# A three-block layer at width 1024: the order of TensorE's queue at the norm boundaries

## The chip, the cores and the metric

One core of a Trainium2 chip runs the whole program. The metric is the device time of one execution in microseconds (us); the median of several executions stands for a kernel.

## The reference

A sequence of 512 tokens of width 1024 passes two blocks, all in fp32. Every projection is preceded by an RMS norm, whose statistic is a mean of squares over the 1024 features of a token.

```
# first block (16 meta tokens are put in front of the 512)
h = concat([meta, x])
z = rmsnorm(h) @ w_in                      # a, q, k, v, r, lr, ga, gb
y_a = (pool means of a, mixed per group) @ w_pool_out
o = gated linear attention(q, k, v, lr)    # chunks of 64, 4 heads
o = rmsnorm(o) * silu(r);  y_b = o @ w_gla_out
h = h + (sigmoid(ga) * y_a + sigmoid(gb) * y_b) @ w_out
h = h + square(relu(rmsnorm(h) @ w_ff1)) @ w_ff2
x = rmsnorm(h)[16:]
# second block
p = rmsnorm(x) @ w_in_first                # convolution branch and RWKV-7 branch
x = x + rmsnorm(concat([conv(p), rwkv7(p)]) @ w_out)
x = x + rmsnorm(cross attention(rmsnorm(x), mem) @ wo)
x = x + rmsnorm(swiglu(rmsnorm(x)))
```

## The kernel before, in words

Activations lie with features on the partitions: F(i) is a slot of 128 features by 512 tokens. A weight matrix is streamed in units of up to 128 x 2048 values by SyncE, into two raw buffers. Each unit is split by ScalarE (a rounded copy, `wh`) and VectorE (the remainder, `wl`) in pieces of 1024 columns; activations are split the same way, and a product of 128 x 128 by 128 x 512 is made of three matmuls. So a tile (128 output features, 8 steps of k) is 24 matmuls, and a tile of `go` (4 steps of k) is 12. The three matmuls stand in `dense`.

`schedule()` writes one list of steps, and every engine walks it and issues those steps for which it has a function. The order on each engine is thus fixed by hand. `tile` puts the two halves of a tile's matmuls and then its eviction (`ev.<tag>`); `pair` puts two tiles with k as the outer loop, and `pair_end` their evictions. `next_unit` starts a unit: it puts the loads of the two units behind it and the splits of this unit and the next one. Background work (pooling, gated linear attention, convolution taps, the RWKV recurrence, cross attention) is made of generators, and `step` moves each by some yields after every half tile; `drain` runs them to their end. `take` and `rel` hand out the eight PSUM banks in turn, D for dense tiles and M for background work; the first matmul into a bank waits for the eviction of the bank's last user.

A norm is not applied to the operand but to the output of the next projection, so that the dense tiles need not wait for it; their evictions do. A statistic has four parts. ScalarE squares a feature tile, and GpSimd adds the squares into one 128 x 512 sum (`squares`, `add_squares`). `cols` lets TensorE sum over partitions, with 8 short instructions of one column each; VectorE adds epsilon and GpSimd takes the power of -1/2. `spread` lets TensorE lay the result out over all partitions (8 matmuls of 128 columns), and ScalarE copies it to SBUF, where the evictions read it.

The places that the change touches:

- The start: pair 0 of unit `a`, the narrow matmuls of the 16 meta columns (`mmm`, 24 for each tile), `in.rs` (the statistic of the tokens) and `in.rm` (that of the meta columns).
- The boundary `gb` to `go`: after `drain`, the four steps `og` multiply the attention output by its gate (VectorE), round it (ScalarE) and make the remainder (VectorE): the operands `in.os` of `go`. The eviction `ev.go` is a VectorE multiply, a GpSimd add, a ScalarE copy and a VectorE remainder, which is the operand `in.m` of `wo`; SyncE then reloads x into the slot.
- The boundary `wo` to `f1`, with the statistic `ffn.rs`.
- The boundary `f2` to `p`, with `mid.a` and `mid.b`; the second is the norm of a normed value, and `midb` combines the two on VectorE and GpSimd. The steps `x2` scale the eight slots on VectorE, and SyncE stores them.

Of the kernel before, what the change touches and what calls it, by code (L numbers as in the profile page):

```python
# [178 lines left out]
class Plan:  # L179


    def __init__(self):
        self.steps, self.bank, self.before = [], {}, {}
        self.pools = {"D": [0, 1, 2], "M": [3, 4, 5, 6, 7]}
        self.user = {}
        self.done = set()
        self.bgs, self.pace, self.rate, self.weight = [], {}, 1, {}
        self.unit, self.loaded, self.cut = 0, set(), set()
        self.base = {}
        for n, u in enumerate(UNITS):  # L190
            self.base.setdefault(u[0], []).append(n)
# [9 lines left out]
    def rel(self, pool, *key):  # L201
        self.pools[pool].append(self.bank[key])

# [70 lines left out]
    def pair(self, n, i0, meta=False):  # L274
        tag = UNITS[n][0]
        for j in range(2):
            self.take("D", "t." + tag, i0 + j)
        for k in range(UNITS[n][3]):
            self.put("ko", n, i0, k)
        if meta:  # L280
            for j in range(2):
                self.take("M", "t." + tag + "_m", i0 + j)
                self.put("mmm", n, j, i0 + j)

    def pair_end(self, n, i0, meta=False):
        tag = UNITS[n][0]
        for j in range(2):
            self.put("ev." + tag, i0 + j)
            if meta:
                self.rel("M", "t." + tag + "_m", i0 + j)  # L290
            self.rel("D", "t." + tag, i0 + j)
            self.step()
# [12 lines left out]
def schedule():  # L305
# [9 lines left out]
    def bg_gla():  # L315
# [58 lines left out]
        for h in range(4):  # L374
            put("gla.sq", h)
            yield
            pl.cols(f"gla.n{h}", "M")
            yield
            pl.spread(f"gla.n{h}", "M")
            put("gla.norm", h)  # L380
            yield

# [8 lines left out]
    for k in range(8):  # L391
        put("sq.in", k)
    n = pl.next_unit("a")
    pl.pair(n, 0, meta=True)
    pl.cols("in.rs")
    pl.spread("in.rs")
    pl.cols("in.rm")
    pl.spread("in.rm")
    pl.pair_end(n, 0, meta=True)
# [22 lines left out]
    pl.drain(bgm)  # L422
    pl.begin(bg_gla())
# [28 lines left out]
    for tag, cnt in (("r", 2), ("ga", 4), ("gb", 4)):  # L452
        for uu in range(cnt):
            n = pl.next_unit(tag)
            for j in range(2):
                pl.tile(n, j, 2 * uu + j)
    pl.drain()
    for h in range(4):
        put("og", h)
# [4 lines left out]
    for uu in range(4):  # L464
        n = pl.next_unit("wo")
        for j in range(2):
            pl.tile(n, j, 2 * uu + j)
    put("gfg")
    for g in range(4):
        for uu in range(4):  # L470
            n = pl.next_unit("f1")
            i0 = 8 * g + 2 * uu
            if g == 0 and uu == 0:
                pl.pair(n, i0)
                pl.cols("ffn.rs")
                pl.spread("ffn.rs")
                pl.pair_end(n, i0)
# [16 lines left out]
    pl.spread("mid.a")  # L494
    pl.cols("mid.b")
    put("midb")
    pl.spread("mid.b")
    put("cvz")
    put("pset")
    pl.pair_end(n, 0)  # L500
    p_tile(0)
    p_tile(1)
# [193 lines left out]
    due = None  # L696
    for uu in range(1, 7):
# [130 lines left out]
    def one_bank_set():  # L828
        pl.pools["D"] += pl.pools["M"]
        pl.pools["M"] = []  # L830

    one_bank_set()
# [49 lines left out]
    pl.pools["M"], pl.pools["D"] = pl.pools["D"][3:], pl.pools["D"][:3]  # L882
# [14 lines left out]
    one_bank_set()  # L897
# [45 lines left out]
def program(nc, wstream, vecs, cf, cu, xT, metaT, memT, pmix, gup, wau, gupg, out, x2s, kvs):  # L943
# [5 lines left out]
    with ctx:  # L949
# [718 lines left out]
        def scalar(e):  # L1668
# [20 lines left out]
            def sq_in(k):  # L1689
                squares("in.rs", k, F(k))  # L1690
                squares("in.rm", k, mh[:, k, :])
# [308 lines left out]
            def evh_dn(i, h):  # L2000
# [4 lines left out]
                "split": split, "xs": xs, "ms": ms, "sq.in": sq_in, "spread": spread, "gla.gate": gla_gate,  # L2005
# [530 lines left out]
        def gpsimd(e):  # L2536
# [14 lines left out]
            def sq_in(k):  # L2551
                add_squares("in.rs", k)
                add_squares("in.rm", k)
# [102 lines left out]
            def end_b(_, i, h):  # L2656
# [5 lines left out]
                "cols": cols, "sq.in": sq_in, "gla.prod": gla_prod, "ev.r": ev_r, "ev.ga": ev_ga, "ev.go": ev_go,  # L2662
# [185 lines left out]
```

How the kernel before makes its waits and increments, by code:

```python
    def wait_ge(self, *keys):  # L136
        for key in keys:
            if key is None or self.value is None:
                continue
            sem, n = self.value[key]
            if n > self.seen.get(sem, 0):
                self.seen[sem] = n
                self.raw.wait_ge(self.book.handle(sem), n)
# [1109 lines left out]
            def dense(n, j, b, k, x, N, done=None, c0=0):  # L1253
                _, _, _, nk, _, w, _ = UNITS[n]
                b = b[0:w, c0:c0 + N]
                c = (j * nk + k) * w
                lh, ll = WH[n % 2][:, c:c + w], WL[n % 2][:, c:c + w]
                xh, xl, key = x
                e.wait_ge(("w.lo", n, min(c // 1024, len(cut_list(n)) - 1)), key)
                e.mm(b, lh, xh, start=(k == 0), stop=False)
                e.mm(b, lh, xl, start=False, stop=False)
                t = e.mm(b, ll, xh, start=False, stop=(k == nk - 1))
                if done and k == nk - 1:
                    t.then_inc(*e.up("mm", *done))
# [1 line left out]
            def mm(n, j, i, half):  # L1266
                tag, nk = UNITS[n][0], UNITS[n][3]
                K = ("t." + tag, i)
                if half == 0:
                    e.wait_ge(freed(*K))
                for k in range(nk // 2) if half == 0 else range(nk // 2, nk):
                    dense(n, j, ps(*K), k, operand(tag, i, k), 256 if tag == "km" else 512, K)
# [20 lines left out]
            def mmm(n, j, i):  # L1293
                K = ("t." + UNITS[n][0] + "_m", i)
                e.wait_ge(freed(*K))
                for k in range(8):
```

## Time and profile before

| | us |
|---|---|
| Median of three executions | 1794.6 |
| The three | 1794.26, 1794.6, 1799.52 |
| The profiled execution | 1800.14 |
| Its span, first to last instruction | 1798.0 |
| TensorE busy | 1678.5 |
| VectorE busy | 834.5 |
| ScalarE busy | 604.5 |
| GpSimd busy | 402.2 |

The profiled execution is one of its own, and the device time beside its span has some 2 us of start and end around it. Busy times overlap. The mean granted clock of TensorE over the span was 0.955 of full speed.

### The profile page before, as it was taken

How to read it: one execution, taken by the hardware profiler on the slowest of the kernel's cores; microseconds unless marked ns; L12 is line 12 of the kernel's file. 1: busy time of each engine (PE TensorE's matmuls, PEld its weight loads, DVE VectorE, ACT ScalarE, POOL GpSimd, SP SyncE). 2: the span in 40 equal slices, each digit the busy share in tenths (PEclk: the TensorE clock that was granted, in tenths of full speed). 3: DMA queues.
4: the chain of work that ended last, by engine and by line, in shares of the span. 5: the costliest groups of instructions: out<-in, count | busy, mean ns of one | idle time of the engine just before them, and what ended most of it. 6: DMA issues, size and time to landing. Idle time of an engine off the chain costs nothing.

```text
span 1798.0 us, 26861 instructions
## 1 busy us (share of the span) xinstructions
PE 1678.5 (93%) x11510; PEld 1377.9 (77%) x11510; DVE 834.5 (46%) x1240; ACT 604.5 (34%) x973; POOL 402.2 (22%) x349
## 2 busy tenths in 40 slices
PE   7999999989999999998988877898989899999997
PEld 6789878767788888887776666777859878888876
DVE  3468642345333333344556887635633433233234
ACT  4234332223323232343335442324433423222222
POOL 2102111112201010132034540104203432131133
PEclk8899999999999999998999889898999999999998
DMA  6124311223222222222311100013202222222221
GB/s 213 48 71 147 136 71 47 94 71 117 84 104 87 101 90 98 93 85 90 120 49 48 47 3 2 3 49 131 81 24 71 71 94 94 94 94 94 94 76 65
DMA packets 29829, 146.03 MB, mean 81 GB/s; under 512 B 4096, under 2 KB 7440, under 8 KB 14608
## 3 DMA queue, kind: packets, MB, share of 16 engines
q1 hardware_dynamic: 29712, 144.33, 22.8%
q8 instruction: 91, 1.49, 0.4%
q14 instruction: 26, 0.21, 0.0%
HBM read 138.03 MB, written 6.29 MB: 80 GB/s over the span
## 4 chain that ended last, share of the span: by engine, by line
PE 77%; issue 8%; DVE 7%; POOL 5%; ACT 3%; DMA 0%; POOLq 0%; SPq 0%; DVEq 0%; ACTq 0%
PE ps L153 77%; POOL zf L165 4%; DVE zf L165 2%; DVE zf L173 2%; ACT zf L162 1%; ACT zf L159 1%; POOL tn L165 1%; DVE ps L173 1%; DVE wl L165 1%; ACT zr L162 1%; ACT wh L162 0%; PE ps L156 0%; DVE zf L2292 0%; DMA raw<-in_wstream 0%; DVE zr L173 0%
## 5 line engine op out<-in xcount | busy, mean ns | idle before, releaser
L153 PE MATMUL ps<-zr,wh 128*128 128x512 f32 (+1 forms) x3936 | 1181.6, 385 | 34.0 <-DVE wl L165 13.4
L153 PEld LDWEIGHTS ps<-zr,wh 128*128 128x128 f32 x3936 | 722.4, 192 | 197.0 <-issue 13.3
L153 PE MATMUL ps<-zr,wl 128*128 128x512 f32 (+1 forms) x1968 | 748.9, 381 | 0.0
L165 POOL TENSOR_TENSOR zf<-zf 128x512 f32<-128x512 f32 (+1 forms) x253 | 297.1, 1181 | 869.1 <-ACT zf L159 581.4
L153 PEld LDWEIGHTS ps<-zr,wl 128*128 128x128 f32 x1968 | 376.5, 191 | 77.6
L165 DVE TENSOR_TENSOR wl<-raw,wh 128x1024 fp32r<-128x1024 f32 (+1 forms) x243 | 306.2, 1300 | 231.9 <-ACT wh L162 231.9
L162 ACT ACTIVATE wh<-raw 128x1024 fp32r<-128x1024 f32 (+1 forms) x243 | 240.3, 1037 | 198.4 <-PE ps L153 196.8
L159 ACT ACTIVATE zf<-zf 128x512 f32<-128x512 f32 (+2 forms) x232 | 127.6, 560 | 411.7 <-DVE zf L165 297.2
L153 PE MATMUL ps<-zf 64*64 64x64 f32 (+6 forms) x3640 | 204.1, 248 | 34.6 <-DVE zf L165 18.6
L153 PEld LDWEIGHTS ps<-zf 64*64 64x64 f32 (+3 forms) x3640 | 162.8, 149 | 75.7 <-issue 29.7
L165 DVE TENSOR_TENSOR zf<-ps,zf 128x512 f32<-128x512 f32 (+2 forms) x133 | 84.2, 639 | 214.1 <-PE ps L153 198.3
L162 ACT ACTIVATE zf<-ps 128x512 f32<-128x512 f32 (+2 forms) x160 | 74.1, 482 | 205.2 <-PE ps L153 189.9
L165 POOL TENSOR_TENSOR zr<-zf,zr 128x512 fp32r<-128x512 f32 x54 | 69.8, 1293 | 285.8 <-ACT zr L162 285.8
L165 DVE TENSOR_TENSOR zf<-zf,ps 128x512 f32<-128x512 f32 (+1 forms) x112 | 62.7, 571 | 147.8 <-PE ps L153 146.6
L162 ACT ACTIVATE zr<-zf 128x512 fp32r<-128x512 f32 x74 | 46.4, 631 | 172.9 <-POOL zf L165 144.2
L153 PE MATMUL ps<-cf_sb,zf 64*64 64x64 f32 (+2 forms) x988 | 68.3, 242 | 23.9 <-ACT zf L159 13.2
L153 PEld LDWEIGHTS ps<-cf_sb,zf 64*64 64x64 f32 (+1 forms) x988 | 63.9, 165 | 28.2 <-issue 11.7
L165 POOL TENSOR_TENSOR tn<-tn,cf_sb 128x2 f32<-128x2 f32 (+3 forms) x29 | 31.6, 1090 | 222.7 <-DVE tn L169 130.5
L173 DVE SCALAR_TENSOR_TENSOR zf<-ps,zf 128x512 f32<-128x512 f32 x46 | 31.4, 690 | 98.2 <-PE ps L153 90.8
L162 ACT ACTIVATE zf<-zf,vecs_sb 128x512 f32<-128x512 f32 x73 | 49.7, 716 | 52.4 <-DVE zf L165 44.9
L173 DVE SCALAR_TENSOR_TENSOR zr<-zf,vecs_sb,zr 128x256 fp32r<-128x256 f32 (+1 forms) x64 | 45.5, 720 | 44.6 <-ACT zr L162 44.6
L165 DVE TENSOR_TENSOR zf<-zf 128x512 f32<-128x512 f32 (+4 forms) x91 | 59.6, 666 | 11.3 <-ACT zf L159 10.2
(94 smaller groups left out, 720.2 us busy)
## 6 DMA issues: line engine op xcount, KB each, us to landing
raw<-in_wstream SPq DMA_DIRECT2D x117, 1024.0 KB, 4.8
zf<-in_xT SPq DMA_DIRECT2D x16, 256.0 KB, 2.8
raw<-in_wstream SPq DMA_DIRECT2D x4, 768.0 KB, 4.3
kv_scratch<-zf SPq DMA_DIRECT2D x8, 256.0 KB, 2.2
x_scratch<-zf SPq DMA_DIRECT2D x8, 256.0 KB, 2.1
zf<-x_scratch SPq DMA_DIRECT2D x8, 256.0 KB, 4.5
out<-zf SPq DMA_DIRECT2D x16, 128.0 KB, 1.7
zf<-in_cu SPq DMA_DIRECT2D x1, 1256.0 KB, 9.9
```

Source lines behind the costliest of these rows:

```text
L153: return self.raw.matmul(out_, l, x, start=start, stop=stop)
L159: return self.raw.activation(out_, in_, fn, bias=bias, scale=scale)
L162: return self.raw.activation(out_, in_, mybir.ActivationFunctionType.Copy, scale=scale)
L165: return self.raw.tensor_tensor(out_, a, b, o)
L173: return self.raw.scalar_tensor_tensor(out=out_, in0=a, scalar=s, in1=b, op0=o1, op1=o2)
```

## The change

Bank sets: all eight PSUM banks serve dense tiles where no background work with PSUM runs (from the start to the end of `q`, and from `go` through the first two units of `p`), where before three did. `two_bank_sets` and `one_bank_set` switch.

The start: the squares of the tokens are all made before those of the meta columns, on ScalarE and GpSimd. The column sums of `in.rs` stand right behind the first pair, and the narrow matmuls of the two tiles stand between the statistics' steps.

`og` is made by the background generator of the attention, one head a step, once `r` is there. The first two tiles of `wo` are a `pair`.

`ffn.rs`, `mid.a` and `mid.b`: after the first pair the column sums follow at once, and the spreads are put between the half tiles of the second unit, whose matmuls now stand ahead of the first pair's evictions. So four tiles wait for their evictions there. `x2` stands behind the evictions of four `p` tiles instead of two.

```diff
@@ -181,7 +181,7 @@
 
     def __init__(self):
         self.steps, self.bank, self.before = [], {}, {}
-        self.pools = {"D": [0, 1, 2], "M": [3, 4, 5, 6, 7]}
+        self.pools = {"D": list(range(8)), "M": []}
         self.user = {}
         self.done = set()
         self.bgs, self.pace, self.rate, self.weight = [], {}, 1, {}
@@ -200,6 +200,13 @@
 
     def rel(self, pool, *key):
         self.pools[pool].append(self.bank[key])
+
+    def two_bank_sets(self):
+
+        self.pools = {"D": self.pools["D"][:3], "M": self.pools["D"][3:]}
+
+    def one_bank_set(self):
+        self.pools = {"D": self.pools["D"] + self.pools["M"], "M": []}
 
     def mark(self, *key):
         self.done.add(key)
@@ -271,23 +278,17 @@
         self.rel("D", "t." + tag, n, i)
         self.step()
 
-    def pair(self, n, i0, meta=False):
+    def pair(self, n, i0):
         tag = UNITS[n][0]
         for j in range(2):
             self.take("D", "t." + tag, i0 + j)
         for k in range(UNITS[n][3]):
             self.put("ko", n, i0, k)
-        if meta:
-            for j in range(2):
-                self.take("M", "t." + tag + "_m", i0 + j)
-                self.put("mmm", n, j, i0 + j)
-
-    def pair_end(self, n, i0, meta=False):
+
+    def pair_end(self, n, i0):
         tag = UNITS[n][0]
         for j in range(2):
             self.put("ev." + tag, i0 + j)
-            if meta:
-                self.rel("M", "t." + tag + "_m", i0 + j)
             self.rel("D", "t." + tag, i0 + j)
             self.step()
 
@@ -379,6 +380,11 @@
             pl.spread(f"gla.n{h}", "M")
             put("gla.norm", h)
             yield
+        while not has(("r",)):
+            yield
+        for h in range(4):
+            put("og", h)
+            yield
 
     put("pro")
     for k in range(8):
@@ -388,15 +394,22 @@
             pl.split(0)
     for k in range(8):
         put("ms", k)
-    for k in range(8):
-        put("sq.in", k)
+    for what in ("sq.in", "sq.im"):
+        for k in range(8):
+            put(what, k)
     n = pl.next_unit("a")
-    pl.pair(n, 0, meta=True)
+    pl.pair(n, 0)
     pl.cols("in.rs")
-    pl.spread("in.rs")
-    pl.cols("in.rm")
+    for j in range(2):
+        pl.take("D", "t.a_m", j)
+        put("mmm", n, j, j)
+        if j == 0:
+            pl.cols("in.rm")
+            pl.spread("in.rs")
     pl.spread("in.rm")
-    pl.pair_end(n, 0, meta=True)
+    pl.pair_end(n, 0)
+    for j in range(2):
+        pl.rel("D", "t.a_m", j)
     n = pl.next_unit("a")
     for j in range(2):
         pl.tile(n, j, 2 + j, meta=True)
@@ -420,6 +433,7 @@
     for j in range(2):
         pl.tile(n, j, j)
     pl.drain(bgm)
+    pl.two_bank_sets()
     pl.begin(bg_gla())
     for uu in range(2):
         n = pl.next_unit("v")
@@ -454,14 +468,17 @@
             n = pl.next_unit(tag)
             for j in range(2):
                 pl.tile(n, j, 2 * uu + j)
+        mark(tag)
     pl.drain()
-    for h in range(4):
-        put("og", h)
+    pl.one_bank_set()
     for uu in range(2):
         n = pl.next_unit("go")
         for j in range(4):
             pl.tile(n, j, 4 * uu + j)
-    for uu in range(4):
+    n = pl.next_unit("wo")
+    pl.pair(n, 0)
+    pl.pair_end(n, 0)
+    for uu in range(1, 4):
         n = pl.next_unit("wo")
         for j in range(2):
             pl.tile(n, j, 2 * uu + j)
@@ -473,8 +490,17 @@
             if g == 0 and uu == 0:
                 pl.pair(n, i0)
                 pl.cols("ffn.rs")
-                pl.spread("ffn.rs")
-                pl.pair_end(n, i0)
+                first = n
+                continue
+            if g == 0 and uu == 1:
+                for j in range(2):
+                    pl.take("D", "t.f1", 2 + j)
+                    put("mm", n, j, 2 + j, 0)
+                    if j == 0:
+                        pl.spread("ffn.rs")
+                    put("mm", n, j, 2 + j, 1)
+                pl.pair_end(first, 0)
+                pl.pair_end(n, 2)
                 continue
             for j in range(2):
                 pl.tile(n, j, i0 + j)
@@ -491,15 +517,25 @@
     n = pl.next_unit("p")
     pl.pair(n, 0)
     pl.cols("mid.a")
-    pl.spread("mid.a")
     pl.cols("mid.b")
     put("midb")
-    pl.spread("mid.b")
     put("cvz")
     put("pset")
-    pl.pair_end(n, 0)
-    p_tile(0)
-    p_tile(1)
+    n = pl.next_unit("p")
+    pl.take("D", "t.p", 2)
+    put("mm", n, 0, 2, 0)
+    pl.spread("mid.a")
+    put("mm", n, 0, 2, 1)
+    pl.take("D", "t.p", 3)
+    put("mm", n, 1, 3, 0)
+    pl.spread("mid.b")
+    put("mm", n, 1, 3, 1)
+    for i in range(4):
+        put("ev.p", i)
+        pl.rel("D", "t.p", i)
+        if i:
+            p_tile(i - 1)
+    pl.two_bank_sets()
     for i in range(8):
         put("x2", i)
 
@@ -693,8 +729,8 @@
     prep = bg_prep()
     pl.pace[prep] = 3
     pl.begin(prep, bg_head(0, 0), bg_head(0, 1), bg_head(1, 0), bg_head(1, 1), bg_fin())
-    due = None
-    for uu in range(1, 7):
+    due = 3
+    for uu in range(2, 7):
         if uu == PFIRST:
             for i in range(4):
                 n = pl.next_unit("cv")
@@ -825,11 +861,7 @@
         some(1, 1, 4, 5, 6, 7)
         pl.spread(new + "1")
 
-    def one_bank_set():
-        pl.pools["D"] += pl.pools["M"]
-        pl.pools["M"] = []
-
-    one_bank_set()
+    pl.one_bank_set()
     for j in range(4):
         put("ev.wb", j)
         pl.rel("D", "t.wb", j)
@@ -879,7 +911,7 @@
         put("ev.wq", j)
         mark("q", j)
         pl.rel("D", "t.wq", j)
-    pl.pools["M"], pl.pools["D"] = pl.pools["D"][3:], pl.pools["D"][:3]
+    pl.two_bank_sets()
     pl.rate = 1
     for uu in range(2, 4):
         n = pl.next_unit("wq")
@@ -894,7 +926,7 @@
             pl.rel("D", "t.wq", i)
             pl.step()
     pl.drain()
-    one_bank_set()
+    pl.one_bank_set()
     for uu in range(2):
         n = pl.next_unit("xo")
         for j in range(2):
@@ ScalarE (GpSimd's add_squares is divided the same way) @@
             def sq_in(k):
                 squares("in.rs", k, F(k))
+
+            def sq_im(k):
                 squares("in.rm", k, mh[:, k, :])
```

## Rows read from the trace of the kernel before

**Rows 1.** The page: busy time by engine; the chain that ended last.

```profile
PE 1678.5 (93%) x11510; PEld 1377.9 (77%) x11510; DVE 834.5 (46%) x1240; ACT 604.5 (34%) x973; POOL 402.2 (22%) x349
...
PE 77%; issue 8%; DVE 7%; POOL 5%; ACT 3%; DMA 0%; POOLq 0%; SPq 0%; DVEq 0%; ACTq 0%
```

**Rows 2.** Timeline of TensorE: start, us, form, count, [idle before <- releaser].

```profile
329.65 1.13 PE L153 MATMUL ps<-cf_sb,tn 128*128 128x128 f32 x8 [1.18 <-POOL tn L165]
...
467.25 0.95 PE L153 MATMUL ps<-cf_sb,zf 128*128 128x1 f32 x8
...
469.64 1.54 PE L153 MATMUL ps<-cf_sb,tn 128*128 128x128 f32 x8 [1.44 <-POOL tn L165]
...
471.86 1.22 PE L153 MATMUL ps<-zr,wh 128*128 128x512 f32 x2 [0.69 <-ACT zf L162]
```

**Rows 3.** Windows of 1 us: busy by engine, PEclk (granted clock), DMA share, GB/s.

```profile
26.00:27.00 1.00, 1.00 (x9) 1.00 (x8) 0.45 (x1) 1.00 (x2) 0.73 (x2) 0.73 0.00 0
...
40.00:41.00 1.00, 1.00 (x6) 0.81 (x5) 0.36 (x1) 0.00 (x0) 0.00 (x0) 0.94 0.00 0
...
412.00:413.00 1.00, 0.00 (x0) 0.00 (x0) 0.12 (x1) 0.78 (x2) 0.18 (x1) 0.59 0.26 100
...
470.00:471.00 1.00, 1.00 (x7) 0.88 (x6) 0.00 (x0) 0.00 (x0) 0.00 (x0) 0.60 0.00 0
...
477.00:478.00 1.00, 1.00 (x5) 0.80 (x5) 1.00 (x2) 0.01 (x1) 0.00 (x0) 0.99 0.00 0
...
849.00:850.00 1.00, 1.00 (x6) 0.82 (x5) 1.00 (x3) 0.92 (x1) 0.00 (x0) 0.96 1.01 373
```

**Rows 4.** Windows of whole stretches, same columns.

```profile
315.00:333.00 18.00, 16.74 (x84) 13.46 (x84) 8.14 (x10) 5.06 (x8) 5.57 (x4) 1.00 0.27 94
...
474.00:832.00 358.00, 358.00 (x1530) 287.47 (x1530) 131.24 (x134) 115.99 (x150) 62.93 (x46) 1.00 0.26 93
...
900.00:1235.00 335.00, 287.12 (x4642) 237.50 (x4642) 219.51 (x391) 131.90 (x239) 100.14 (x73) 0.92 0.10 35
```

**Rows 5.** Timeline of TensorE at the mid boundary.

```profile
832.70 0.95 PE L153 MATMUL ps<-cf_sb,zf 128*128 128x1 f32 x8
...
841.68 2.04 PE L153 MATMUL ps<-cf_sb,tn 128*128 128x128 f32 x8 [2.30 <-DVE zf L2216]
...
844.41 1.22 PE L153 MATMUL ps<-zr,wh 128*128 128x512 f32 x2 [0.69 <-ACT zf L162]
```

**Rows 6.** Timeline of VectorE behind the mid boundary.

```profile
845.94 6.72 DVE L173 SCALAR_TENSOR_TENSOR zf<-zf,vecs_sb 128x511 f32<-128x511 f32 x10 [0.19 <-ACT zf L162]
```

**Rows 7.** Timeline of TensorE at the go boundary.

```profile
375.64 0.70 PE L153 MATMUL ps<-zr,wh 128*128 128x512 f32 x2 [2.86 <-DVE zr L165]
...
381.53 1.22 PE L153 MATMUL ps<-zr,wh 128*128 128x512 f32 x2 [0.35 <-DVE zr L165]
...
410.29 0.73 PE L153 MATMUL ps<-zr,wh 128*128 128x512 f32 x2 [1.67 <-DVE zr L165]
...
413.63 1.22 PE L153 MATMUL ps<-zr,wh 128*128 128x512 f32 x2 [2.37 <-DVE zr L165]
```

**Rows 8.** Timeline of VectorE around the go boundary.

```profile
331.45 0.75 DVE L173 SCALAR_TENSOR_TENSOR zf<-zf,vecs_sb 128x512 f32<-128x512 f32 x1 [1.68 <-ACT zf L162]
...
384.00 0.69 DVE L165 TENSOR_TENSOR zf<-ps,zf 128x512 f32<-128x512 f32 x1
...
422.65 0.69 DVE L165 TENSOR_TENSOR zf<-zf,ps 128x512 f32<-128x512 f32 x1 [3.81 <-PE ps L153]
```

**Rows 9.** Timeline of TensorE at the start.

```profile
29.05 1.84 PE L153 MATMUL ps<-cf_sb,zf 128*128 128x1 f32 x8
...
37.08 1.22 PE L153 MATMUL ps<-zr,wh 128*128 128x512 f32 x2 [0.27 <-ACT mrs L162]
```

**Rows 10.** Timeline of GpSimd at the start: first and seventh add of 512 columns.

```profile
16.69 1.32 POOL L165 TENSOR_TENSOR zf<-zf 128x512 f32<-128x512 f32 x1 [16.26 <-ACT zf L159]
...
25.28 1.27 POOL L165 TENSOR_TENSOR zf<-zf 128x512 f32<-128x512 f32 x1
```

More of the change, by code:

```diff
@@ L2004, in scalar @@
             run(e, {
-                "split": split, "xs": xs, "ms": ms, "sq.in": sq_in, "spread": spread, "gla.gate": gla_gate,
+                "split": split, "xs": xs, "ms": ms, "sq.in": sq_in, "sq.im": sq_im, "spread": spread, "gla.gate": gla_gate,
                 "gla.log": gla_log, "gla.exp": gla_exp, "gla.ends": gla_ends, "gla.turn": gla_turn,
@@ L2552, in sq_in, with sq_im @@
                 add_squares("in.rs", k)
+            def sq_im(k):
                 add_squares("in.rm", k)
@@ L2661, in gpsimd @@
             run(e, {
-                "cols": cols, "sq.in": sq_in, "gla.prod": gla_prod, "ev.r": ev_r, "ev.ga": ev_ga, "ev.go": ev_go,
+                "cols": cols, "sq.in": sq_in, "sq.im": sq_im, "gla.prod": gla_prod, "ev.r": ev_r, "ev.ga": ev_ga, "ev.go": ev_go,
                 "ev.wo": ev_wo, "ev.f1": ev_f1, "ev.f2": ev_f2, "midb": midb, "tap.g": tap_g, "conv.sq": conv_sq,
```

## The prediction

> **What bounds the kernel now.** I read the page first: TensorE is busy 93% of a span of 1798.0 us, and 77% of the chain that ended last is its matmuls; no other engine is busy half of the time, VectorE 46% [rows 1]. So time is won where TensorE stands still or runs at the lower clock, and both are to be looked up stretch by stretch. The timeline of TensorE with its idle times [rows 2] shows at four places of the change a chain that is always the same: short column sums, a pause, a spread, a pause, dense matmuls. The windows of 1 us beside it give the granted clock, 1.00 (2.4 GHz) or 0.50 (1.2 GHz); a value between the two tells when it switched (0.60 in 470 to 471 is a fall at 470.2) [rows 3]. The dense matmul of 512 columns starts every 0.233 us at the upper level and every 0.427 us at the lower, so each us of work at 0.50 is worth 0.5 us.
>
> **The change part by part.** I count from start to start, because modelled ends overlap the pauses by 0.1 to 0.2 us.
>
> *The ffn boundary.* Column sums start at 467.25, dense work is back at 471.86, the clock fell at 470.2 and came back at 477.02 [rows 2, 3]. The stretch 467.25 to 477.02 is 9.77 us. Its content at 1.00 is 0.95 (column sums) + 1.13 (a spread at full clock, that of 329.65 in [rows 2]) + 5.16 x 0.5 = 2.58 of dense work, 4.66 together. The new order has between the sums and the spread a half tile of 2.8 us (12 x 0.233), more than the pause of 1.44 between them; the next half covers the 0.69 of the copy. So no pause is left, and 9.77 - 4.66 = **5.1 us** go. That the clock holds when column sums and spreads lie between dense work is what 315 to 333 shows, where the statistics of the gated operand run that way at 1.00, with a pause of 1.18 us besides [rows 2, 4]. ScalarE and VectorE: the split of the next unit now stands ahead of the spread's copy, 2.0 us on ScalarE, under the 2.8 us of the half tile. The four tiles' evictions wait for the copy, and need four of the eight banks, the two statistics two more: no bank wait.
>
> *The mid boundary.* The same twice in a row: 832.70 to 849.08 is 16.38 us [rows 3, 5]. At full clock and without pauses it is 0.95 + 1.13 + 0.95 + 1.13 + 4.67 x 0.5 = 6.5 us. The second statistic's chain of small operations (VectorE, GpSimd, VectorE) took 2.30 us after its sums; in the new order 2.8 + 1.13 + 5.6 us of TensorE work cover it. Gain 16.38 - 6.5 = **9.9 us**. What is late next: VectorE. It now has four evictions, three mixes and the eight scalings of x2 behind the last spread, and the split for the first cv unit behind those. By the new order the last spread's copy lands at about 845.9; four evictions and three mixes (0.65 each with the copies between) take it to 850.6, eight scalings at 0.67 (ten operations in 6.72) [rows 6] to 856.0, the split's first half to 857.2. TensorE wants it at 832.70 + 1.9 + 2.3 + 22.4 = 859.3. So 2.1 us are left, and I cost this at nothing; if it is later the surplus is paid. SyncE: the store of x2 follows the scalings and is done some 2 us after 856, before the gates of the background (they follow tile 5, 859). The load of the second cv unit stands behind these stores, at 856 with over 10 us until it is wanted.
>
> *The go boundary.* Before: gb's matmuls end at about 372.6; the gated operand needs four rounds VectorE, ScalarE, VectorE of 2.0 us (375.64 to 381.53 in three of them), then the split of the second go unit, and only then, at 384.00, comes the first eviction of go [rows 7, 8]. TensorE waits four times there, 2.86 us first and 0.35 last, 4.9 in all. From 384.00 on the chain eviction, GpSimd add, ScalarE copy, VectorE remainder takes 3.36 us a tile, slower than TensorE's 2.8: eight of them and a split (2.6 more) put the last remainder at 413.6. TensorE waits 1.67 and 2.37 us for the last two operands, 0.3 once for a bank, and the clock is down from 412.18 [rows 3, 7]. The first pair of wo tiles ends at 422.6, with the eviction at 422.65 [rows 8]. After: the statistics behind the gated operand end at 332 [rows 8], and 40 us of gb lie behind it with VectorE busy about as on the whole page [rows 1], so the four rounds (8 us) fit there. Then at 372.62 go starts at once. VectorE: eviction of gb until 373.5, sigmoid, split of go's second unit (ScalarE from 374.15, VectorE until 377.5), first eviction at 377.5 instead of 384.00, hence the whole chain 6.5 us earlier and its last operand at 407.1. TensorE: eight go tiles until 395.0 without a bank wait, then the wo pair in order of k: k = 0 to 5 until 403.4, k = 6 wants the operand of 403.7, k = 7 that of 407.1, end at 408.5. Two pauses of 0.3 and 2.0 us. Gain 422.6 - 408.5 = **14.0 us**. Bounds: if the clock falls in those pauses, as it did after 1.67 us with 2.37 behind it, some 2.7 us come back (5.4 us at the lower level); if the chain keeps its old time, 7 us are left. On SyncE the reload of x and the loads keep their order and move with the chain.
>
> *The start.* This part goes the other way. Before, the pair ended at 22.54, the narrow matmuls of the meta rows filled until 29.05, and the sum of squares was ready at 26.55, when nobody waited for it [rows 9, 10]. Now the column sums come straight behind the pair. GpSimd's adds of 512 columns take 1.27 us each without the small ones between (they start 1.43 apart with them, 16.69 to 25.28 in six steps); the first can start at 16.6, the seventh ends at about 25.4. So TensorE now waits 22.54 to 25.4, **2.9 us** that were not there. Then 0.95 (sums), 24 narrow matmuls, 0.2 (the other sums, whose small adds take 7 x 0.5 us and are done by 29), a spread, 24 narrow ones, a spread of 0.57. All pauses of before (1.44, 0.69, 0.95, 0.27) are gone, but the clock fell at 26.46, 3.9 us into the narrow matmuls, and a pause in their place gives it no reason to stay up. At 0.50 a narrow one takes 0.213 us (0.112 at 1.00): 25.4 + 1.0 + 5.1 + 0.2 + 2.05 + 5.1 + 0.6 = 39.4, where dense work resumed at 37.08. Dense work then needs 3.0 to 5.4 us until the clock is back (37.08 to 40.12, 471.86 to 477.02, 844.41 to 849.08); before it was the least of these, so I add 0.7. Cost **+3.0 us**. Bounds: +4, and -5 if the clock holds all along (the same sum with 0.112 and 1.13 ends at 33.3).
>
> Sum: -5.1 - 9.9 - 14.0 + 3.0 = **-26.0 us**. Between the boundaries TensorE has no idle time in 474 to 832 [rows 4], and the stage behind mid keeps its order on each engine, so the shifts pass through. Against the profiled execution's 1800.1 this is 1774.1; the median of the runs shown, 1794.6, is 5.5 lower, and the same difference gives **1769** (1768.6).
>
> **The clock, rule against row.** The Trainium skill (TensorE: Matmul & The Clock Gate, "HAM oscillation") lets only pauses longer than any here re-throttle the array. By that rule the falls at 470.2 and 412.18 are no result of the pauses, and removing them would give back idle time alone; the sum would be that of the first rival below. The trace speaks against it, since the clock fell at 470.2 with pauses of 1.44 and 0.69 us and column sums as the only difference from the 350 us around it.
>
> **The rivals.**
> *The clock goes down all the same* (column sums and spreads are narrow and still there). Then only idle time is saved: 2.1 at ffn, 5.1 at mid, 9.3 - 2.4 at go, 0.5 at the start, 14.6 in all: 1780. For it: the fall at 26.46, during narrow matmuls without any pause. Against: the 1.00 of 315 to 333 [rows 4]. Chance 0.12.
> *VectorE takes back what mid gives*: the cv split late by the evictions, then the taps and the recurrence, where TensorE waits mostly for VectorE, start no earlier. Then 9.9 are lost: 1779. For it: only 2.1 us of slack. Chance 0.10.
> *The gated operand is not earlier*, because the background ends too late. Then go gains only by banks and by the order of k: the last operand at 413.6, the pair's end at 415.5 to 416, 6.5 instead of 14.0: 1776. Against: 332 lies 40 us ahead of 372. Chance 0.03.
> *The start gains too*, the clock holding: 1761. Chance 0.07.
> *Slower*: the recurrence stage, 900 to 1235, runs thin matmuls at a mean clock of 0.92 with TensorE busy 287 of 335 us [rows 4]. Its clock hangs on when its bursts fall, and a shift moves them. The work is 287 x 0.92 = 264 us of full clock; a mean of 0.84 would need 314, 27 us more, and from there on the kernel is slower. For it: the stage has pauses all along. Against: its order on every engine stays, so its pauses should too. Chance 0.03.
> The likeliest has 0.62, the rest (no change to be seen, nothing of these) 0.03.
>
> **How the numbers follow.** The likeliest's own range is 1762 to 1776: go 10 to 14, ffn and mid less 2 together, start +4 to 0, and the clock of the recurrence. The range that holds 8 in 10 takes in the idle-only case and most of the start's gain: 1758 to 1783. A difference of 0.3% (5.4 us) is about what can be told from none. Faster 0.94, same 0.03, slower 0.03.
>
> **What would show it.** Right: no pause of TensorE over 0.3 us and a clock of 1.00 behind the column sums of ffn and mid; the first go matmul right behind gb, one pause of 2 us in the wo pair; a new pause of about 3 us ahead of the first column sums, with GpSimd's add as releaser, and dense work back later than 37.08. Wrong: lower clock at ffn or mid with no pause; a wait for a weight remainder at the first cv unit; a stage from cv to the out projection that is longer than before.

## The result and the profile after

The changed kernel's median is 1774.06 us (four executions, 1769.49 to 1775.78), beside 1796.55 for the kernel before (four, 1794.26 to 1799.52). The ratio is 0.987, 95% interval 0.9844 to 0.9896. The profiled execution took 1775.8 us with a span of 1773.7. A second set of four gave 1776.06 and 0.9887 (0.9858 to 0.9916). The forecast was 1769, with 1758 to 1783 as its range.

The page of the changed kernel, the same two lines as [rows 1]: TensorE is busy 8.7 us less and the span is 24.3 us shorter. So 15.6 us of the gain are idle time, and 8.7 are mostly matmuls that ran at the upper clock, since their number is the same.

```profile
PE 1669.8 (94%) x11510; PEld 1373.4 (77%) x11510; DVE 835.0 (47%) x1240; ACT 605.4 (34%) x973; POOL 401.6 (23%) x349
...
PE 75%; DVE 8%; issue 7%; POOL 5%; ACT 4%; DMA 1%; POOLq 0%; SPq 0%; DVEq 0%; ACTq 0%
```

*ffn and mid.* TensorE's timeline at both boundaries, against [rows 2, 5]. No row has an idle time any more: sums, half a tile, spread. The 16 instructions at 817.54 are both statistics' sums.

```profile
457.38 0.95 PE L153 MATMUL ps<-cf_sb,zf 128*128 128x1 f32 x8
...
461.07 1.05 PE L153 MATMUL ps<-cf_sb,tn 128*128 128x128 f32 x8
```

```profile
817.54 1.84 PE L153 MATMUL ps<-cf_sb,zf 128*128 128x1 f32 x16
...
822.13 1.05 PE L153 MATMUL ps<-cf_sb,tn 128*128 128x128 f32 x8
...
828.60 1.05 PE L153 MATMUL ps<-cf_sb,tn 128*128 128x128 f32 x8
```

The windows of the changed kernel (columns as in [rows 3]): the clock is 1.00 at both boundaries, and TensorE is busy all of the time. The first two windows belong to the start (a fall at 26.24, a return at 46.72), the last is the recurrence stage. Between 135.5 and 855.7 us this trace has no stretch at the lower clock at all.

```profile
26.00:27.00 1.00, 0.63 (x3) 0.63 (x4) 0.00 (x0) 0.22 (x1) 0.67 (x3) 0.62 0.00 0
46.00:47.00 1.00, 1.00 (x5) 0.78 (x4) 0.00 (x0) 0.00 (x0) 0.00 (x0) 0.64 1.01 147
462.00:480.00 18.00, 18.00 (x80) 14.48 (x79) 5.96 (x7) 8.71 (x13) 6.43 (x5) 1.00 0.30 107
817.00:835.00 18.00, 18.00 (x96) 15.18 (x95) 7.86 (x23) 6.55 (x10) 2.03 (x2) 1.00 0.03 13
880.00:1212.00 332.00, 287.31 (x4603) 237.51 (x4600) 217.80 (x390) 127.89 (x232) 95.66 (x71) 0.91 0.10 32
```

VectorE behind mid, against [rows 6]: the eight scalings (with one mix ahead of them) end at 840.8, and the weights' remainder for the first cv unit is made from 840.75, its first half by 842.0. TensorE wants it at 844.2. The slack forecast as 2.1 us is 2.2.

```profile
834.79 6.05 DVE L173 SCALAR_TENSOR_TENSOR zf<-zf,vecs_sb 128x511 f32<-128x511 f32 x9
840.75 2.36 DVE L165 TENSOR_TENSOR wl<-raw,wh 128x1024 fp32r<-128x1024 f32 x2
```

*go.* VectorE's timeline: the last eviction of gb, the split, the first eviction of go 4.62 us behind the former, where it was 11.18 [rows 8]. TensorE has one pause of note left, ahead of k = 7 of the wo pair (one of 0.13 us stands ahead of k = 6), and the clock stays at 1.00.

```profile
376.69 0.69 DVE L165 TENSOR_TENSOR zf<-ps,zf 128x512 f32<-128x512 f32 x1 [4.91 <-PE ps L153]
379.03 2.36 DVE L165 TENSOR_TENSOR wl<-raw,wh 128x1024 fp32r<-128x1024 f32 x2 [1.65 <-ACT wh L162]
381.31 0.68 DVE L165 TENSOR_TENSOR zf<-ps,zf 128x512 f32<-128x512 f32 x1
```

```profile
410.93 0.73 PE L153 MATMUL ps<-zr,wh 128*128 128x512 f32 x2 [1.70 <-DVE zr L165]
```

*The start.* TensorE's timeline, against [rows 9]. The first pair ends at 23.92. There is the new pause, 2.29 us as the row tells and 2.45 from start to start, released by GpSimd's add. Everything behind it is slow: the narrow matmuls start every 0.213 us, and dense work is back at 41.49.

```profile
23.69 0.39 PE L153 MATMUL ps<-zr,wl 128*128 128x512 f32 x1
26.37 1.86 PE L153 MATMUL ps<-cf_sb,zf 128*128 128x1 f32 x8 [2.29 <-POOL zf L165]
28.10 0.36 PE L153 MATMUL ps<-muh,wh 128*128 128x16 f32 x1
...
34.03 2.08 PE L153 MATMUL ps<-cf_sb,tn 128*128 128x128 f32 x8 [0.52 <-POOL tn L165]
...
41.49 1.22 PE L153 MATMUL ps<-zr,wh 128*128 128x512 f32 x2
```

The chain that ended last, in order of time, shows what sets that stretch (start, us, what). GpSimd's adds of 512 columns start every 1.43 us, the same as before with the small ones between them [rows 10], so the last ends at 26.3. And a second chain hangs on the first: the small squares follow the adds, the split of the next unit follows the small squares on ScalarE, and VectorE makes its remainder (2.36 us) before it comes to the epsilon of the first statistic, whose power starts at 32.96, though its sums were done at 28.1.

Eight traces have this start: the two of the changed kernel and those of the six runs below that keep it. This chain is of one length in all of them: the spread starts 7.7 us behind the end of the last large add, and dense work 7.5 us behind the spread. The moment at which the clock falls is not: from 0.1 us ahead of the column sums (here) to 2.8 us behind their start. Where it falls late, the first narrow matmuls are done sooner and TensorE waits longer ahead of the spread, up to 3.00 us instead of 0.52. So up to the spread it is the chain that costs, and not the clock.

```profile
16.46 1.30 POOL zf L165
...
25.06 1.26 POOL zf L165
...
29.26 0.21 ACT msq L159
29.47 0.95 ACT wh L162
30.45 2.36 DVE wl L165 x2
32.96 1.03 POOL tn L165
```

Distances between marks in the traces, one execution each. "gb" is the start of the last gb eviction, "ffn" and "mid" the starts of their column sums, "heads" the first per-head sum of the recurrence (128x2), "end" the end of the span:

| | start to gb | gb to ffn | ffn to mid | mid to heads | heads to end |
|---|---|---|---|---|---|
| before | 372.8 | 94.4 | 365.5 | 47.7 | 917.6 |
| changed | 376.7 | 80.7 | 360.2 | 37.4 | 918.8 |
| changed, second trace | 376.5 | 80.7 | 360.2 | 37.8 | 912.6 |
| change | +3.9, +3.7 | -13.7 | -5.3 | -10.3, -9.9 | +1.2, -5.0 |
| forecast | +3.0 | -14.0 | -5.1 | -9.9 | 0 |

### The profile page after: what moved, and what is told of

It is laid out like the page before. It is cut to its first block, busy times and chain, and to the rows that moved or that the text cites. A ratio compares the mean times of both kernels' runs of the same rounds, so it can differ in the third digit from the quotient of the medians.

```text
span 1773.7 us, 26856 instructions
## 1 busy us (share of the span) xinstructions
PE 1669.8 (94%) x11510; PEld 1373.4 (77%) x11510; DVE 835.0 (47%) x1240; ACT 605.4 (34%) x973; POOL 401.6 (23%) x349
## 4 chain that ended last, share of the span: by engine, by line
PE 75%; DVE 8%; issue 7%; POOL 5%; ACT 4%; DMA 1%; POOLq 0%; SPq 0%; DVEq 0%; ACTq 0%
PE ps L153 75%; POOL zf L165 4%; DVE zf L165 2%; DVE zf L173 2%; DVE wl L165 1%; ACT zf L159 1%; ACT zr L162 1%; DVE ps L173 1%; ACT zf L162 1%; DMA raw<-in_wstream 1%; POOL tn L165 1%; ACT wh L162 1%; PE ps L156 0%; DVE zf L2326 0%; DVE zr L173 0%
## 5 line engine op out<-in xcount | busy, mean ns | idle before, releaser
L153 PE MATMUL ps<-cf_sb,zf 64*64 64x64 f32 (+2 forms) x988 | 68.8, 247 | 25.4 <-ACT zf L159 13.2
L153 PEld LDWEIGHTS ps<-cf_sb,zf 64*64 64x64 f32 (+1 forms) x988 | 64.4, 169 | 29.9 <-issue 11.6
```

The costliest lines, as they stand in the source:

```text
L153: return self.raw.matmul(out_, l, x, start=start, stop=stop)
```

## The experiments

All are edits of the changed kernel. They were timed against the kernel before in three sets; the second trace above is of the third set. Executions of one kernel lie up to 10 us apart (1790.89 to 1800.49 for the kernel before). Much of it arises in one place: "heads to end" reads 912 to 919 us over all fourteen traces, with the same order of work. So the distances ahead of it are compared in the traces, and medians only say what reaches the end.

### The start put back

```diff
-    for what in ("sq.in", "sq.im"):
-        for k in range(8):
-            put(what, k)
+    for k in range(8):
+        put("sq.in", k)
+        put("sq.im", k)
...
-    pl.cols("in.rs")
...
-        if j == 0:
-            pl.cols("in.rm")
-            pl.spread("in.rs")
+    pl.cols("in.rs")
+    pl.spread("in.rs")
+    pl.cols("in.rm")
```

> The changed kernel with the start alone put back (squares interleaved, both meta tiles ahead of the column sums, spreads without work between them; eight banks stay). Theory (the new start costs 3 to 4 us: a pause for the sum of squares, and narrow matmuls at the lower clock behind it): dense work resumes 14.5 us after the end of the first pair instead of 18.0, and the median is about 1770.5, 3.5 us below the changed kernel's 1774.1. Rival (the later marks of the changed kernel's trace come from where the clock happened to switch in that one execution, the first pair itself having ended 1.4 us later): 1774, no difference beyond 1 us.

Measured: 1767.59 us (1766.58 to 1769.34), ratio 0.9842 (0.9827 to 0.9856). TensorE's timeline: pair's end 22.85, sums at 28.58, dense work back at 35.39, the second tile of the second unit at 46.35, which the changed kernel starts at 52.16.

```profile
31.77 2.08 PE L153 MATMUL ps<-cf_sb,tn 128*128 128x128 f32 x8 [1.35 <-POOL tn L165]
...
35.39 1.22 PE L153 MATMUL ps<-zr,wh 128*128 128x512 f32 x2
...
46.35 0.70 PE L153 MATMUL ps<-zr,wh 128*128 128x512 f32 x2
```

The new start costs: start to gb is 370.9 here, 376.2 to 378.9 in the eight traces with the new start, and the median is 6.5 us lower than the changed kernel's first and 8.5 lower than its second. The rival, a chance of the clock in one trace, falls. The forecast of 3.5 was too small: dense work is back 12.5 us after the pair's end, not 14.5, since the eight banks stay in this run and the kernel before's pauses of 0.69 and 0.27 us are not in its timeline.

### Statistics late, under the second unit

```diff
-    pl.cols("in.rs")
...
-        if j == 0:
-            pl.cols("in.rm")
-            pl.spread("in.rs")
+    pl.cols("in.rs")
+    pl.cols("in.rm")
+    first = n
+    n = pl.next_unit("a")
...
+    put("mm", n, 0, 2, 0)
+    pl.spread("in.rs")
+    put("mm", n, 0, 2, 1)
...
-    pl.pair_end(n, 0)
+    put("mmm", n, 0, 2)
+    pl.pair_end(first, 0)
```

> The changed kernel with another start: squares interleaved, pair, both meta tiles, both column sums, then the spreads between the half tiles of the second unit. Theory (statistics cost nothing where dense work covers them and the sum of squares is ready): no pause, dense work 8.6 us after the end of the pair, with about 2.6 us of spreads inside it; about 7 us below the changed kernel, 1767, and 3 us below the kernel with the start put back. Rival (the narrow meta tiles keep the clock down whatever follows, or the second unit's weights come late): as the kernel with the start put back, 1770 to 1771.

Measured: 1767.24 us (1763.85 to 1769.19), ratio 0.9837 (0.982 to 0.9853). Timeline, sums to second tile:

```profile
31.89 1.84 PE L153 MATMUL ps<-cf_sb,zf 128*128 128x1 f32 x8
...
33.81 1.22 PE L153 MATMUL ps<-zr,wh 128*128 128x512 f32 x2
...
39.09 1.43 PE L153 MATMUL ps<-cf_sb,tn 128*128 128x128 f32 x8
...
46.27 0.83 PE L153 MATMUL ps<-zr,wh 128*128 128x512 f32 x2
```

No pause is left, and yet the second tile starts at 46.27, as with the start put back. The sums came 3.3 us later than there. Of this 1.1 us is the pair's own end, and the rest is the clock: it fell 2.3 us into the narrow matmuls here, at 26.2, so that 27 of the 48 ran at 0.50, and 4.8 us into them there, at 27.6, with 5 at 0.50. In the run of both improvements below, with the same start, it fell at 28.5, and that tile started at 42.79. So the theory is right about the pauses, and its 3 us below the start put back are not seen: the medians are equal. How many narrow matmuls run at the lower clock is worth as much, and one trace cannot tell the two apart.

### The sum of squares over half the features

The squares and adds of four of the eight feature tiles are left out, so the statistic is of half the features; all else is as in the changed kernel.

```diff
+            if s == "in.rs":
+                return (s + ".acc", 3)
...
+                if s == "in.rs" and n > 3:
+                    return
...
-                if n and not (n == 7 and s in LATE):
+                if n and not (n == 7 and s in LATE) and not (s == "in.rs" and n > 3):
```

> The changed kernel with the sum of squares of the tokens taken over four of the eight feature tiles (the other four squares and adds left out), so that the sum is there before the first pair ends; order of TensorE's queue as in the changed kernel. Theory (the pause ahead of the column sums is the wait for GpSimd, and narrow matmuls behind dense ones bring the clock down by themselves): no pause, but the clock still falls within 4 us, and dense work is back 13 to 15.5 us after the end of the pair, where the changed kernel has 17.6 and the kernel before 14.5; 1771. Rival (the pause brought the clock down): the clock holds, dense work back after 9 us, 1766.

Measured: 1765.7 us (1764.06 to 1768.42), ratio 0.983 (0.9804 to 0.9857).

```profile
28.37 1.64 PE L153 MATMUL ps<-cf_sb,tn 128*128 128x128 f32 x8 [1.03 <-POOL tn L165]
...
35.39 1.22 PE L153 MATMUL ps<-zr,wh 128*128 128x512 f32 x2
...
45.37 0.71 PE L153 MATMUL ps<-zr,wh 128*128 128x512 f32 x2
```

The pause ahead of the sums is gone: they start right behind the pair, at 23.58. So that pause was the wait for the add. The clock still falls, at 28.9, and dense work is back at 35.39, 11.8 us after the pair's end: 17.6 in the changed kernel, 13 to 15.5 by the theory, 9 by the rival. The median is at the rival's 1766 and not at the theory's 1771, though the clock did not hold as the rival wants.

What brought the clock down isn't settled by this run: 24 narrow matmuls passed at the upper clock, from 24.4 to 27.1, and the fall comes 0.5 us behind the pause of 1.03 us ahead of the spread. The traces with all 48 in a row and no pause among them show that narrow matmuls are enough: the clock fell 3.9 us into them in the kernel before, 4.8 with the start put back, 2.3 with the late statistics and 5.1 in the run of both improvements. And the pause ahead of the sums is not what decides in the changed kernel: in seven of the eight traces with its start the clock was still at 1.00 when the sums began.

### The gated operand where it was

```diff
-        while not has(("r",)):
-            yield
-        for h in range(4):
-            put("og", h)
-            yield
...
     pl.drain()
+    for h in range(4):
+        put("og", h)
     pl.one_bank_set()
```

> The changed kernel with the gated operand made where it was, between gb and go; eight banks and the pair of wo stay. Theory (four rounds of 2.0 us stand between gb and go, VectorE's eviction chain starts 6.5 us later, and the clock falls): TensorE waits 4.9 us ahead of go, the pair of wo ends 6.5 to 9 us later than in the changed kernel, 1781 to 1783. Rival (banks and order of k carry the gain of this boundary): 1774 to 1776.

Measured: 1780.35 us (1777.88 to 1781.87), ratio 0.9915 (0.99 to 0.993). The four pauses of [rows 7] are back, first and last:

```profile
381.07 0.70 PE L153 MATMUL ps<-zr,wh 128*128 128x512 f32 x2 [2.86 <-DVE zr L165]
...
386.95 1.22 PE L153 MATMUL ps<-zr,wh 128*128 128x512 f32 x2 [0.34 <-DVE zr L165]
```

gb to ffn is 87.3 us instead of 80.7: 6.6, at the lower end of what was expected.

### wo without the pair

```diff
-    n = pl.next_unit("wo")
-    pl.pair(n, 0)
-    pl.pair_end(n, 0)
-    for uu in range(1, 4):
+    for uu in range(4):
```

> The changed kernel with the first two tiles of wo one after the other again. Theory (the last operand comes at about the same time, but 6.3 us of dense work stand behind it instead of 1.4): the second wo tile ends 4.9 us later, up to 7.5 with a fall of the clock in the longer pauses; 1779 to 1781. Rival (what is waited for here is made up until the f1 boundary): 1774.

Measured: 1778.61 us (1774.82 to 1782.58), ratio 0.9907 (0.9882 to 0.9932). Three pauses, 5.7 us, and the clock at 0.50 from 404.8 to 415.1:

```profile
403.72 0.73 PE L153 MATMUL ps<-zr,wh 128*128 128x512 f32 x2 [1.66 <-DVE zr L165]
...
407.05 1.22 PE L153 MATMUL ps<-zr,wh 128*128 128x512 f32 x2 [2.36 <-DVE zr L165]
...
410.39 1.22 PE L153 MATMUL ps<-zr,wh 128*128 128x512 f32 x2 [1.69 <-DVE zr L165]
```

gb to ffn is 87.5: 6.8, between the 4.9 and the 7.5 expected.

### Three banks in go and wo

```diff
     pl.drain()
-    pl.one_bank_set()
...
     put("gfg")
+    pl.one_bank_set()
```

> The changed kernel with three banks for dense tiles in go and wo, eight from f1 on. Theory: with the eviction chain at 3.36 us a tile the eighth go tile waits 1.8 us for a bank, and the pair of wo must wait for the eviction of the seventh go tile, 4.7 us ahead of its place in the chain; the pair ends 2.8 us later, 1777. Rival (banks don't matter, the chain sets the end in any case): 1774.

Measured: 1777.21 us (1772.65 to 1777.56), ratio 0.9893 (0.9876 to 0.991). The two waits for an eviction, at the eighth go tile and in the pair:

```profile
399.41 0.73 PE L153 MATMUL ps<-zr,wh 128*128 128x512 f32 x2 [1.85 <-DVE zf L165]
...
406.11 0.73 PE L153 MATMUL ps<-zr,wh 128*128 128x512 f32 x2 [1.40 <-DVE zf L165]
```

gb to ffn is 83.5: 2.8, as worked out. The three undoings add to 16.2 for a gain of 13.7. So a part is worth a little more beside the others than alone, and each of the three traces has a fall of the clock in this stretch (383.5 to 390.3, 404.8 to 415.1, 400.4 to 403.8) that the changed kernel has not.

### The ffn statistic where it was

```diff
                 pl.cols("ffn.rs")
-                first = n
-                continue
...
-                    if j == 0:
-                        pl.spread("ffn.rs")
...
+                pl.spread("ffn.rs")
+                pl.pair_end(n, i0)
```

> The changed kernel with the statistic of ffn in its old place, two pauses and no dense work between sums and spread. Theory (pauses of 1.44 and 0.69 us and a fall of the clock to 0.50 for 6.8 us): f2 begins 5.1 us later, 1779. Rival (the clock falls for another reason, only idle time is given up): 2.1 us, 1776.

Measured: 1775.95 us (1770.24 to 1778.62), ratio 0.9881 (0.986 to 0.9903), which is not apart from the changed kernel's. In the trace ffn to mid is 363.3 against 360.2, so 3.1 us, between the theory's 5.1 and the rival's 2.1. The windows show the clock fall at 462.4, 3.9 us after the sums began, and return at 465.8; the timeline shows one pause and no second one behind the spread.

```profile
462.00:463.00 1.00, 1.00 (x5) 0.82 (x4) 0.19 (x1) 0.60 (x1) 0.00 (x0) 0.71 0.00 0
465.00:466.00 1.00, 1.00 (x4) 0.79 (x3) 0.00 (x0) 0.97 (x3) 1.00 (x1) 0.59 0.00 0
```

```profile
460.94 1.13 PE L153 MATMUL ps<-cf_sb,tn 128*128 128x128 f32 x8 [1.44 <-POOL tn L165]
461.82 0.71 PE L153 MATMUL ps<-zr,wh 128*128 128x512 f32 x2
```

So one pause of 1.44 us, with the column sums ahead of it and the spread behind it, was enough for a fall. It had been so in the kernel before: the clock fell at 470.2 and at 835.4, in the spread, and the pause of 0.69 us came only after that. The length of the pause isn't what decides: the pause of 1.70 us in the wo pair, between dense matmuls, left the clock at 1.00 in all seven traces that have it there. The 0.69 of [rows 2] is not there, though the order is that of before: the dense tile no longer waits for the copy once it has eight banks to start in. The account closes: 1.44 and half of 3.4 us at the lower clock are 3.1. In the kernel before it was 1.44 + 0.69 and half of 6.8, 5.5. So of the 5.3 us won here, the order is worth 3.1 in this trace, and the rest is the second pause, which the banks took, and a longer stretch at the lower clock, which may be chance.

### The mid statistics where they were

```diff
     pl.cols("mid.a")
+    pl.spread("mid.a")
     pl.cols("mid.b")
     put("midb")
+    pl.spread("mid.b")
...
-    due = 3
-    for uu in range(2, 7):
+    due = None
+    for uu in range(1, 7):
```

> The changed kernel with the two statistics of mid in their old place: four pauses between sums and spreads, two p tiles ahead of x2. Theory: the first cv unit begins 9.9 us later, of which 8.8 arrived behind the gates of the recurrence; 1783. Rival (the clock falls for another reason, only idle time is given up): 5.1 us, 1779. Second rival (the recurrence stage takes the gain back): 1775.

Measured: 1781.39 us (1776.3 to 1782.7), ratio 0.9911 (0.9883 to 0.9939). Mid to heads is 44.1 against 37.4 and 37.8, so 6.3 to 6.7 us, with the clock down from 824.6 to 831.4:

```profile
824.00:825.00 1.00, 0.00 (x0) 0.00 (x0) 0.31 (x2) 0.00 (x0) 0.57 (x1) 0.80 0.00 0
831.00:832.00 1.00, 1.00 (x5) 0.79 (x4) 1.00 (x2) 0.97 (x2) 0.00 (x0) 0.79 0.00 0
```

Less than the 10.3 of the first pair of traces for the same two reasons: the pauses are 1.44 and 2.30 in its timeline and the two of 0.69 are gone, and it has 6.8 us at 0.50 where the kernel before had 13.7. 3.7 and half of 6.8 are 7.1, against 6.3 to 6.7 measured. The median moves by 5.3 and 7.3 us against the changed kernel's two, so the stage behind takes nothing back.

### The eviction of go pipelined

```diff
                 e.tt(F(i), ps("t.go", i)[:, :], F(i), MUL).then_inc(*e.up("t.go", i))
+                if i:
+                    go_lo(i - 1)
+
+            def go_lo(i):
                 lo(("in.m", i), R(16 + i), F(i), R(8 + i), "in.mh2", i)
```

> The changed kernel with VectorE's eviction of go pipelined: the multiply of tile i stands ahead of the remainder of tile i-1, so VectorE no longer waits for GpSimd and ScalarE within a tile. Theory (the pause of 1.7 us in the first pair of wo and the 0.3 us before it come from that chain's pace of 3.36 us a tile): both pauses gone, about 2 us less, 1772. Rival (the split of the next wo unit, or its load, behind the chain sets the end): pause moves, no gain.

Measured: 1773.34 us (1771.66 to 1774.84), ratio 0.9872 (0.9858 to 0.9887). VectorE's timeline, a remainder behind the next tile's multiply:

```profile
397.07 0.68 DVE L165 TENSOR_TENSOR zr<-zf,zr 128x512 fp32r<-128x512 f32 x1
397.67 0.68 DVE L165 TENSOR_TENSOR zf<-ps,zf 128x512 f32<-128x512 f32 x1
399.60 1.10 DVE L165 TENSOR_TENSOR zr<-zf,zr 128x512 fp32r<-128x512 f32 x1 [1.25 <-ACT zr L162]
```

TensorE has no pause from gb to f1, and gb to ffn is 78.2: 2.5 us less, about 2 expected. The median is 0.7 and 2.7 us under the changed kernel's two, at the edge of what it can tell.

### Both improvements together

```diff
+    n = pl.next_unit("a")
...
+    pl.spread("in.rs")
...
+    put("go.lo", 7)
...
+                if i:
+                    go_lo(i - 1)
```

> Both of these together: the late-statistics start and the pipelined eviction of go. Theory: the gains add, 9 us below the changed kernel, 1765. Rival (what the start gives is lost again in the recurrence stage, where TensorE mostly waits for others): 1770 or more.

Measured: 1763.54 us (1758.82 to 1766.71), ratio 0.9816 (0.9796 to 0.9836), in one set with the pipelined eviction alone (1773.34) and the late statistics alone (1767.24). The windows of this kernel are read in the next part.

### The narrow matmuls dealt out

```diff
+    for k in range(8):
+        put("ko", n, 0, k)
+        if k >= 4:
+            for j in range(2):
+                for kk in (2 * k - 8, 2 * k - 7):
+                    put("mk", n, j, j, kk)
...
+        for k in range(8 if meta else 0):
+            self.put("kt", n, j, i, k)
+            self.put("mk", n, j, i, k)
```

> The late-statistics start with the pipelined eviction of go, and the narrow matmuls of the meta rows dealt out between dense ones (24 of a tile among the dense matmuls, three behind each step of k) instead of in runs of 24 and 48. Same matmuls, other order. Theory (the clock falls because narrow matmuls stand in runs): no fall before 60 us, where the run before had about 15 us at 0.50; 5 to 7 us less, 1757. Rival (narrow matmuls lower the clock wherever they stand, or cost their place between dense ones): 1763 or more.

Measured: 1757.65 us (1750.97 to 1759.53), ratio 0.9777 (0.9747 to 0.9808). Windows with the narrow matmuls dealt out, then one of the run before, which has them in runs:

```profile
29.00:30.00 1.00, 1.00 (x8) 0.86 (x7) 1.00 (x2) 0.68 (x1) 1.00 (x2) 0.93 0.37 92
36.00:37.00 1.00, 1.00 (x7) 1.00 (x6) 0.00 (x0) 0.00 (x0) 0.00 (x0) 0.65 0.06 25
37.00:60.00 23.00, 23.00 (x135) 20.15 (x135) 7.83 (x16) 4.14 (x11) 2.32 (x3) 1.00 0.13 46
```

```profile
37.00:60.00 23.00, 23.00 (x114) 19.36 (x113) 5.41 (x12) 3.90 (x11) 2.36 (x3) 0.85 0.14 51
```

From 37 us on the clock stays at 1.00 with 24 narrow matmuls among each tile's dense ones, where it was 0.85 on the mean. One fall is left, from 29.9 to 36.7, behind the second half of the first pair, where 12 narrow ones stand behind every six dense ones, and the sums after it; so "no fall before 60 us" was not met. The mark gb is at 362.4 instead of 368.6, 6.2 us, and the median falls by 5.9. It is the best version of all, 2.2% below the kernel before.

### The changed kernel again

> The changed kernel once more, beside the others on one chip: 1774, its start as in the first trace up to where the clock switches (a pause of 2.3 to 2.9 us ahead of the column sums).

Measured: 1776.06 us (1769.85 to 1776.41), ratio 0.9887 (0.9858 to 0.9916). The pause is 3.56 us in that trace, beyond the 2.3 to 2.9 expected: the pair ended 1.8 us sooner and the last add only 0.5.

## Why the prediction was right, point by point

**go, -14.0: right, -13.7.** TensorE's pair of wo ended 14.1 us sooner against the gb mark, with the pause of 2 us where it was put (1.70 by the row) and 0.13 us for the 0.3 ahead of it. VectorE was freer in the 40 us of gb than the page's mean, at which it was taken: busy 12.1 us of them. The parts were sized by undoing: 6.6 for the operand's place, 6.8 for the order of k, 2.8 for the banks.

**ffn, -5.1, and mid, -9.9: right (-5.3, -10.3), for the mechanism named, but not by the order alone.** Pauses and the clock went, both terms. The prediction gave them all to the dense work put between sums and spread. The undone orders show 3.1 and 6.3 to 6.7 for it; the pauses of 0.69 (one at ffn, two at mid) go by the eight banks. The time at the lower clock, 3.4 for 6.8 us and 6.8 for 13.7, is shorter in the runs with fewer pauses, but one trace each doesn't tell that from chance: the fall itself came 3.0 us after the sums began in one kernel and 3.9 in the other, with the same work up to it.

**The start, +3.0: right in sign, too small.** This is the term of the sum that was mis-sized. The pause ahead of the sums was forecast as 2.9 us and is 2.45 to 3.8 from start to start in the eight traces with this start. Dense work was to be back 16.9 us after the pair's end; it was 17.6 to 19.0. For the clock's later return 0.7 was put, and 1.1 measured in the first trace (5.2 us behind the dense start instead of 3.0, at half value). Two things were missed. The adds' pace did not go from 1.43 to 1.27 when the small adds left: it stayed 1.43, so the sum was there at 26.3 and not at 25.4. And the epsilon of the first statistic had the next unit's split ahead of it on VectorE, so a pause stood ahead of the spread, where the prediction had none: 0.52 us in the first trace, up to 3.00 in the others. From the end of the last add to dense work it is 15.2 us in all eight, where the prediction has 14.0. In the mark, the cost is 3.4 to 6.1 us against the one trace of before, all above the forecast. Against the start put back it is 5.3 to 8.0, and 6.5 to 8.5 in the medians, beyond the upper bound of 4; but that kernel has the eight banks at its start, which the one before has not.

**The stage behind mid, 0: right on the mean.** 917.6 before, 912.1 to 919.3 in the others. It scatters by 7 us with nothing changed in it; what a shift does to it isn't told apart from that.

**From the sum to the forecast.** The sum was -26.0 and the profiled executions differ by 24.4 (1800.1 and 1775.8), 1.6 off. The other 3.8 of the 5.5 us between 1768.6 and 1774.06 come from the last step: it took the profiled execution to stand 5.5 us above the median, from three executions, and took the same for the changed kernel. Further executions put the kernel before at 1795.8 to 1797.7, and the changed kernel's profiled one stood 1.7 above its median. Against those medians the gain is 22 us, 4 less than the sum. The start was mis-sized by 0.4 to 3.1 us of it, against the one trace of before; the rest isn't told apart from the scatter between executions. That the sum came within 1.6 us on the first pair of traces is in part luck: the second trace of the changed kernel has a span 30.3 us shorter than the one of before.

**The rivals.** The clock going down all the same: no, 1.00 at go, ffn and mid. VectorE taking mid back: no, 2.2 us of slack. The gated operand not earlier: no. The start gaining: no, a loss. Slower by the recurrence's clock: no, its window's mean is 0.91 for 0.92, over nearly the same work.

**The clock, rule against row.** At ffn the clock fell behind one pause of 1.44 us, in the kernel before and in the order put back, and held in the changed kernel, where dense work lies between; at the start of the kernel before it fell with no pause, behind narrow matmuls. The rule of the Trainium skill (TensorE: Matmul & The Clock Gate, "HAM oscillation") that the prediction weighed, by which pauses as short as these don't re-throttle the array, isn't borne out by these rows.

## What to carry to other kernels

Put a statistic's cross-partition steps between dense tiles, but only where the sum is ready: ahead of them stands the slowest adder, and a queue that waits for it has lost what followed as cover. Look at what stands between a sum and its spread on the other engines, too: here a weight split on VectorE. Look for narrow matmuls in runs and deal them out among dense ones, which was worth 5.9 us here. A chain of engines behind each tile (here multiply, add, copy, remainder) is paced by its latency when one engine holds two of its links in order; swap the links of neighbouring tiles (2.5 us here, with eight banks already there).

## What the runs showed of the hardware

The granted clock fell behind narrow work alone. In four traces 48 matmuls of 16 columns stand in a row behind the first pair, TensorE busy all of the time, and it went from 1.00 to 0.50 2.3 us (26.2, late statistics), 3.9 (26.5, before), 4.8 (27.6, start put back) and 5.1 us (28.5, both improvements) into them. Three of them behind every three dense ones did not bring it down, over 23 us.

A single pause of 1.44 us between eight column sums and a spread was followed by a fall, too (470.2 and 835.4 before, 462.4 with the ffn statistic put back). Pauses of 1.67 to 1.70 us between dense matmuls in the wo pair were not, in seven traces; one of 1.85 us in go was (400.4, three banks). What exactly tells these apart stays open.

The moment of the fall isn't fixed by the program. Behind the same work it came 3.0 and 3.9 us after the sums of ffn began (467.25 to 470.2, 458.55 to 462.4), 2.7 and 5.4 at mid (832.70 to 835.4, 819.18 to 824.6), and 2.3 and 5.1 us into the narrow matmuls with the same start.

GpSimd's adds of 512 columns kept their 1.43 us from start to start whether an add of 16 columns (0.22 us) stood between them or not.
